# The first projection in quarters, three places of the attention stage in another order, and the last pair's down products in three parts, in a two-layer transformer kernel

## What is computed

```
mp = adaln(cond_ctx, ada_w[l], ada_b[l]);  ms = adaln(c, ada_w[l], ada_b[l])
hp = modulate(xp, norm_mix[l], mp[0], mp[1])          # hs the same with ms
qp, kp, vp, up = attn_pool_project(hp, a_w_in[i], ...)  # z = h @ w_in; q, k, v, u = split(z)
op = concatenate([attention(...), multiscale_pool(up, ...)]) @ a_w_out[i]   # or fourier_mix
xp = xp + mp[2] * op
hp = modulate(xp, norm_ffn[l], mp[3], mp[4])
xp = xp + mp[5] * hier_moe(hp, ...)
    # h1 = x@w1[e]; h3 = x@w3[e]; a = silu(h1)*h3*comb; y = sum over e of a@w2[e]
```

## Time and profile before

| | |
|---|---|
| median of 3 runs | 832.01 us (831.92 to 832.39) |
| the profiled execution: own time | 833.7 us |
| its span (first to last instruction) | 831.9 us |
| TensorE busy | 777.5 us (93%) |
| DVE, ACT busy | 328.9 us, 177.4 us |
| read from HBM | 275.04 MB |

### The profile page before, as it was taken

One profiled execution on the slowest core, in us unless ns is written; L12 is line 12 of the kernel. 1 busy time (PEld: TensorE's weight loads), 2 busy tenths in 40 slices (PEclk: granted clock), 3 DMA queues, 4 the chain that ended last, 5 costly groups with the idle time before them and its releaser, 6 DMA issues.

```text
span 831.9 us, 9943 instructions
## 1 busy us (share of the span) xinstructions
PE 777.5 (93%) x3929; PEld 380.6 (46%) x3929; DVE 328.9 (40%) x711; ACT 177.4 (21%) x422; POOL 2.2 (0%) x9
## 2 busy tenths in 40 slices
PE   3799989999899999999988999999899999999986
PEld 0454444544543444344333657645544444444332
DVE  0305047314732643445315312225832644445306
ACT  2301355403621111111112501104511101110100
POOL 0000000000000000000000000000000000000000
PEclk9899999999999999999999999999999999999999
DMA  8979599932779999999999962022499999999992
GB/s 368 400 271 428 191 430 403 422 141 85 282 269 422 420 421 420 421 421 421 422 419 427 430 278 102 1 101 112 193 354 421 421 421 421 421 421 422 420 412 86
DMA packets 39474, 277.44 MB, mean 334 GB/s; under 512 B 8525, under 2 KB 9441, under 8 KB 10497
## 3 DMA queue, kind: packets, MB, share of 16 engines
q1 hardware_dynamic: 39073, 275.28, 80.7%
q10 hardware_dynamic: 288, 1.34, 0.4%
q0 software_dynamic: 64, 0.13, 0.0%
HBM read 275.04 MB, written 1.70 MB: 333 GB/s over the span
## 4 chain that ended last, share of the span: by engine, by line
PE 83%; DMA 8%; DVE 3%; ACT 3%; issue 1%; DVEq 1%; ACTq 0%; SPq 0%
PE bank L1799 25%; PE bank L1815 12%; PE bank L1697 10%; PE bank L1993 6%; DMA ring<-in_moe_w 6%; PE bank L1784 5%; PE bank L1823 5%; PE bank L2122 4%; PE bank L1635 4%; DMA ring<-in_ada_w 2%; PE bank L2143 1%; PE bank L2061 1%; PE bank L1677 1%; PE bank L2040 1%; PE bank L1648 1%
## 5 line engine op out<-in xcount | busy, mean ns | idle before, releaser
L1799 PE MATMUL bank<-ring,Z 128*64 128x512 f32 x1024 | 229.8, 601 | 8.2 <-DMA ring<-in_moe_w 8.2
L1799 PEld LDWEIGHTS bank<-ring,Z 128*64 128x64 f32 x1024 | 75.6, 138 | 147.2 <-issue 143.7
L1815 PE MATMUL bank<-ring,Z 128*64 128x512 f32 x512 | 113.8, 596 | 0.0
L1697 PE MATMUL bank<-ring,T 128*128 128x512 f32 x192 | 83.1, 593 | 1.2 <-ACT T L1077 1.2
L1815 PEld LDWEIGHTS bank<-ring,Z 128*64 128x64 f32 x512 | 35.2, 137 | 68.9 <-issue 68.6
L1338 DVE TENSOR_TENSOR Z<-Z,bank 128x512 f32<-128x512 f32 x16 | 11.0, 688 | 138.7 <-PE bank L1799 138.7
L1635 PE MATMUL bank<-ring,cond 128*32 128x512 f32 x384 | 49.7, 645 | 8.2 <-DMA ring<-in_ada_w 7.9
L1697 PEld LDWEIGHTS bank<-ring,T 128*128 128x128 f32 x192 | 36.2, 190 | 45.6 <-issue 45.6
L1823 PE MATMUL bank<-ys,Cs 128*128 128x512 f32 x192 | 51.9, 405 | 4.4 <-DVE ys L1356 4.4
L1993 PE MATMUL bank<-ring,T 128*128 128x512 f32 (+1 forms) x144 | 53.6, 535 | 2.5 <-ACT T L888 2.5
L1369 DVE TENSOR_TENSOR x<-x,bank 128x512 f32<-128x512 f32 x84 | 52.1, 681 | 0.3
(11 more groups left out here) (224 smaller groups left out, 690.9 us busy)
## 6 DMA issues: line engine op xcount, KB each, us to landing
ring<-in_moe_w SPq DMA_DIRECT2D x192, 1024.0 KB, 15.6
ring<-in_ada_w SPq DMA_DIRECT2D x24, 2048.0 KB, 13.8
ring<-in_a_w_in SPq DMA_DIRECT2D x2, 2048.0 KB, 33.5
ring<-in_a_w_out SPq DMA_DIRECT2D x2, 2048.0 KB, 11.6
ring<-in_f_w_in SPq DMA_DIRECT2D x2, 2048.0 KB, 28.9
ring<-in_f_w_out SPq DMA_DIRECT2D x2, 2048.0 KB, 27.2
special<-in_att_const SPq DMA_DIRECT2D x1, 1792.0 KB, 9.3
x<-in_x_sample SPq DMA_DIRECT2D x2, 512.0 KB, 21.6
```

The source lines that it names most:

```text
L1697: last = pe.matmul(b[:, :], T[:, k, i * P:(i + 1) * P], w[:, k, :], start=(k == 0), stop=(k == KT - 1))
L1799: last = pe.matmul(out[BLK * u:BLK * (u + 1), :], xT[:, b, k, s0 + BLK * u:s0 + BLK * (u + 1)], w[:, k, :], start=(k == 0), stop=(k == KT ...
L1815: last = pe.matmul(psD[hh][BLK * u:BLK * (u + 1), :], aT[:, k, BLK * u:BLK * (u + 1)], w2[:, FC * hh + k, :], start=(k == 0), stop=(k == F ...
```

## The change

**The start in quarters.** The host puts the columns of `ada_w` in another order: each of the four chunks of a norm now holds shift and scale of one quarter (256) of the model's columns. After each chunk, `ada_read` on DVE does reduce, bias and gain at once for its quarter; `first_affine(j, t)` writes two of the eight column blocks of `T`, and `z_part(j, i)` does the two products that use them, in three banks that accumulate over the four quarters. The first column chunk of `a_w_in` is 512 wide (the second 256), is item 1 of the ring, and is loaded in four parts, each behind the chunk of `ada_w` with the same number; chunk 0 comes in two halves, and the two sample tiles of `x` go ahead of chunk 1. Six products on zeros that are used by nobody stand before and among the first real ones: three of 512 columns before the condition's transposes, two of 256 behind them, and two (256 and 512) around the first `ada_read`.

**The attention stage.** Chunk 4's product stands right behind `z`, ahead of the pooled branch. k is transposed and copied ahead of q, and each first score waits only for its own part of q. Chunks 7 and 8 both stand behind the first scores as before, but ACT copies chunk 7 between the two groups of `exps`; chunk 8 is read after `scores(1, 0)`; chunks 9 and 10 are read inside `values`, between transposes and products.

**The last pair.** Down products in three parts of 512, 256 and 256 columns, the third into the bank `psA`. The part-0 back products stand in the middle of part 2. DVE's and ACT's steps follow the parts. Both layers have it.

```diff
+END_PARTS = [(0, HALF), (HALF, HALF + HALF // 2), (HALF + HALF // 2, D)]
-W_IN_COLS = [256, 512, 512]
+W_IN_COLS = [512, 256, 512]
...
+            sp.dma_start(ring[:, 0, 0:SLOT // 2], before0[0][:, 0:SLOT // 2]).then_inc(ada_first, 16)
+            sp.dma_start(ring[:, 0, SLOT // 2:], before0[0][:, SLOT // 2:]).then_inc(arrived[0], 16)
+            z_part(0)
+            for t in range(1, NT):
+                sp.dma_start(x[:, t, :], x_sample[0, (t - 1) * P:t * P, :]).then_inc(x_in[t], 16)
+            for j in range(1, 4):
+                weights(j + 1, before0[j + 1])
+                z_part(j)
...
+                f, k0 = cc // 6, 2 * (cc % 6)
+                m = mcol[:, l, f, k0:k0 + 2]
+                emptied_inc(dve.tensor_reduce(m.rearrange("p k v c -> p (k v) c"), src, AX.X, ALU.add))
+                settle()
+                bias = bcol[:, (6 * l + 3 * f) * KT:(6 * l + 3 * f + 2) * KT].rearrange("p (v k) -> p k v", v=2)
+                dve.tensor_tensor(m, m, bias[:, k0:k0 + 2, :].unsqueeze(3).to_broadcast([P, 2, 2, 2]), ALU.add)
+                settle()
+                at = (R_MIX, R_FFN)[f] + l * KT + k0
+                gain = colv[:, at:at + 2].unsqueeze(2).to_broadcast([P, 2, 2])
+                dve.scalar_tensor_tensor(m[:, :, 1, :], m[:, :, 1, :], 1.0, gain, ALU.add, ALU.mult).then_inc(affine_ready, 1)
...
             exps(0, 0)
+            ada_product(7)
             exps(0, 1)
-            ada(7, 9)
+            ada_product(8)
             ada_product(9)
...
-                gated_half(s, NPAIR - 1, 2 * BLK, 0)
-                settle()
-                low_half(s, NPAIR - 1, 2 * BLK, 0)
-                last_back(0)
-                last_back(1)
-                gated_half(s, NPAIR - 1, 2 * BLK, 1)
-                last_back(2)
-                settle()
-                low_half(s, NPAIR - 1, 2 * BLK, 1)
+                end_part(gated_part, 0)
+                settle()
+                end_part(low_part_of, 0)
+                end_part(gated_part, 1)
+                last_back(0, 0)
+                end_part(low_part_of, 1)
+                last_back(0, 1)
+                end_part(gated_part, 2)
+                last_back(0, 2)
+                end_part(low_part_of, 2)
                 for i in range(NT):
-                    last_back(NT + i)
+                    last_back(1, i)
+                for i in range(NT):
+                    last_back(2, i)
                     settle()
                     dve.sem_inc(x_ready, 1)
...
+            norm_part(0, 0)
+            ada_product(0)
+            keep_warm(1, HALF // 2)
+            ada_read(0)
+            keep_warm(1)
+            z_part(0, 0)
+            norm_part(1, 0)
+            z_part(0, 1)
+            norm_part(2, 0)
+            ada_product(1)
+            z_part(0, 2)
+            ada_read(1)
+            for j in range(1, 4):
+                z_part(j, 0)
+                if j < 3:
+                    ada_product(j + 1)
+                z_part(j, 1)
+                if j < 3:
+                    ada_read(j + 1)
+                if j == 1:
+                    for i in range(NT):
+                        norm_part(i, 1)
+                z_part(j, 2)
```

More of the change, by code:

```diff
@@ L337, in scores, with values @@
             t.add(("score", i, n), "dve")
-    def values(i, half):
+    def values(i, half, between=None):
         for n in range(4 * half, 4 * half + 4):
             t.add(("PT", i, n), "act")
+        if between:
+            ada_read(between)
         if half:
@@ L1968, in moe @@
                 pair(NPAIR - 1)
+            pe.wait_ge(zeros_ready, 1)
+            for _ in range(3):
+                pe.matmul(banks[7][:, :], zeros[:, 0:P], zeros[:, P:P + HALF], start=True, stop=True)
             pe.wait_ge(small_in, loads[small_in])
@@ L1977, in _, with norm_part @@
             done_by("rows")
-            for n in range(3):
-                ada_product(n)
-                if n > 0:
-                    ada_read(n - 1)
-            norm(0, 0, 1)
-            ada_product(3)
-            ada_read(2)
-            ada_read(3)
-            for cc in range(len(W_IN_COLS)):
+            for _ in range(2):
+                pe.matmul(banks[7][:, 0:HALF // 2], zeros[:, 0:P], zeros[:, P:P + HALF // 2], start=True, stop=True)
+            def norm_part(i, q):
+                pe.wait_ge(normed, i + 1)
+                b = begin(("norm", 0, i, q))
+                for k in range(4):
+                    last = pe.transpose(b[:, k * P:(k + 1) * P], h[:, i, (4 * q + k) * P:(4 * q + k + 1) * P], ident)
+                last.then_inc(full, 1)
@@ new lines, in z_part @@
+            def z_part(j, i):
+                if j < 3:
+                    pe.wait_ge(z_weights[j], 16)
+                    w = ring[:, N_WIN[0], :].rearrange("p (k n) -> p k n", k=KT)
+                else:
+                    w = item(N_WIN[0], W_IN_COLS[0])
+                if i == 1:
+                    pe.wait_ge(first_cols["act"], j + 1)
+                else:
+                    pe.wait_ge(first_cols["dve"], 2 * j + 1 + i // 2)
+                b = begin(("z", 0, i)) if j == 0 else banks[turn[("z", 0, i)][0]]
+                for k in (2 * j, 2 * j + 1):
+                    last = pe.matmul(b[:, :], T[:, k, i * P:(i + 1) * P], w[:, k, :], start=(k == 0), stop=(k == KT - 1))
+                if j == 3:
+                    last.then_inc(full, 1)
```

345 lines of the change are left out of this document (210 added, 135 removed).

## The result

| | before | changed |
|---|---|---|
| median | 832.20 us (831.92 to 832.47, 4 runs) | 818.22 us (817.36 to 818.69, 4 runs) |
| profiled execution: own time, span | 833.7, 831.9 us | 817.36, 815.5 us |

The ratio is 0.9831, with a 95% interval of 0.9814 to 0.9848. The change made the kernel faster, and the time lies in the predicted range (811.5 to 821.5); the forecast of 816.0 was 2.2 us too low. The two profiled spans differ by 16.4 us, close to the forecast sum of 16.0, but partly by luck: one term was 4 us too large, the profiled execution of before is 1.5 us slower than its median, and that of the changed kernel (817.36) is the fastest of its four. The products on zeros that the list of the change calls six are seven: three of 512 columns, two of 256, and one each of 256 and 512.

The account below looks back on a forecast made before the run. TensorE (777.5 of 831.9 us) was taken as the bound, behind a mostly-transfer front of 34.8 us; gains 10.7 + 3.2 + 1.15 + 1.0 = 16.0 us gave 816.0 us, range 811.5 to 821.5.

Parts of the forecast that it names:

- What bounds the start: Start of the kernel: the chain begins with 18.28 us of DMA for `ada_w`; `z` starts only at 34.82 us.
- Term 1: Start in quarters: `z` ends at 78.5 us instead of 89.2, gain 10.7 us, at best 12.7, at worst 6.
- chunk 0 to 12.6 us: Start: TensorE's product of chunk 0, landed at 11.6 us, ends at 12.6, so `z_part(0, 0)` comes at 15.4 us.
- I take full clock: Start in quarters: with pauses of at most 1.6 us and products between them, TensorE is taken to run at full clock.
- the clock goes down in the quarters: Rival at the start: about 7 TensorE pauses between 8 and 26 us cost 2 to 4.5 us: 818 to 820.5; chance 0.18.
- the ring holds: Weight transfers behind the start: item 8 lands at about 55 us, wanted at about 87; nothing is late.
- the lead moves along: Whole kernel: an earlier start of TensorE's dense work moves everything behind it; the expert stream has slack to begin earlier.
- the expert stream does not move along: Rival in the experts: TensorE would wait for just-in-time transfers what it gained, giving 825 to 832 us; chance 0.03.
- Term 2: Attention stage: 4.0 us of TensorE waits removed, less 0.8 for extra DVE steps: gain 3.2 us, bounds 1.0 and 4.5.
- DVE did not become the bound: Rival in the attention stage: DVE is the bound, Term 2 falls to 0.5, time 818.7 us; chance 0.15.
- Term 3: Last pair of both layers: gain 1.15 us at layer 1's end and 1.0 us (bounds 0.3 and 2.8) after layer 0.

Follow-up runs that it names:

- more_dummies: Changed kernel with one more product on zeros ahead of the condition's copies and four instead of two behind: 815.68 us, ratio 0.9803 to the kernel before.

## Why the prediction was right, point by point

**What bounds the start** was read rightly: the transfer of the four chunks ahead of `z` was on the chain, and with quarters TensorE's own work took its place. **Term 1** was mis-sized: 10.7 us forecast, 6.7 measured. Two of its steps failed. The first is "chunk 0 to 12.6 us" and with it "I take full clock": the product ended at 14.6, at half clock, and the first part began at 17.64 instead of 15.4, 2.2 us late; more_dummies won 1.6 of them back. The prediction had assumed that pauses of at most 1.6 us are harmless, from one pause of 1.61 us in the earlier trace rows; here pauses of 0.62 and 0.89 us, with four records on zeros between them, came ahead of it. The second is the price of a part. From the start of a part that stands alone between other work to the start of what follows it, it is 1.79 to 1.88 us (17.64 to 19.43, 29.34 to 31.22), and 1.85 or 1.86 us for a chunk's product (23.36 to 25.22); the sum had 1.72 for each, the time between starts inside a long block. Six such parts cost 0.6 and three chunk products 0.4 of the remaining 1.8 us; the other 0.8 is spread over the small steps between them. Of the rival "the clock goes down in the quarters" only chunk 0 came true, at 1.6 us where its price was 2 to 4.5; the quarters themselves ran at 1.00. That the time of 818.22 us lies in that rival's 818 to 820.5 is chance, since most of what is missing in term 1 has other causes.

The products on zeros, for which the sum gave nothing, were worth 1.7 us of `z`'s end in the one execution without them. There the rule of the Trainium skill's page "TensorE: Matmul & The Clock Gate" (section "What's actually happening"), by which activity lifts the clock from its lower level, points the right way, but the place was another. The 1.3 us that the prediction drew from it for chunk 0 did not show, 3.37 us with them and 3.64 without; 1.0 us showed in the first part, where 4 records took 2.97 us without them and 1.95 with them.

The 6.7 us themselves depend on the two executions: the one of before had half clock at the start of `z`, the one of the changed kernel at chunk 0. Between the executions with the old and with the new start the lead is 4.5 to 8.2 us, and the medians' 6.6 us lie between.

**That the ring holds and that the lead moves along** was right. Every kernel kept at `project(0)` and at the experts of layer 0 what it had won, and the rival "the expert stream does not move along" fell. What the prediction left out is that the experts' time varies by 2 us from execution to execution, in part by one up step at half clock.

**Term 2** was right: 3.2 forecast, 3.7 in the two profiles, with the waits falling as named. DVE did not become the bound, although its own work grew by 3.3 us; a new wait of 0.7 us for it is all. Medians give 4.7 us, just over the upper bound of 4.5; that fits the slow stretch which followed the removed pause of 2.2 us in two of three executions.

**Term 3** was right in sum at the end of layer 1: 1.15 forecast, 1.45 between the two profiles, and 0.9 to 1.4 when the distance from the last down product to the end of the span is taken (8.45 us, against 9.37, 9.85 and 9.42 in the three executions with the old tail). For the start of layer 1 the forecast of 1.0 us names the right mechanism (TensorE is at chunk 20 2.36 us behind the last down product instead of 4.02) and leaves out the clock. With the old tail the distance to `f_w_in` was 15.12 us in the kernel before and 13.27 and 13.28 in the two others; with the new one it is mostly 13.2. TensorE comes to chunk 20 earlier, as forecast, then waits 2.2 us for the first tile, and the clock goes down behind that wait. So by the traces it is 0.1 us where the clock had held before, 1.9 us where it had not, and 0.9 us once the pause is filled.

**Why 14.0 and not 16.0.** The sum was made from the one profiled execution of before, and that execution had bad luck in layer 1: two stretches at half clock at its start (1.85 us, and 0.9 us more up to `project(1)`: 66.55 us against 65.6 in all twelve others) and 222.4 us of experts, with this up step:

```profile
801.57 8.78 PE L1799 MATMUL bank<-ring,Z 128*64 128x512 f32 x32 [3.46 <-DMA ring<-in_moe_w]
```

The changed kernel's profiled execution has the same step at 7.09 us, behind a pause of 2.37. With term 1 at 6.7, the two profiles differ by 6.7 + 3.7 + 0.4 + 1.9 + 0.9 - 0.3 + 2.2 + 0.9 = 16.4 us. Of these, 2.4 are not in the medians: 1.5 because the profile of before is above its median, and 0.9 because that of the changed kernel is below its own. The forecast had taken the sum for a difference of medians. How much the tail is worth in the median is not settled: its 2.9 us (1.4 to 3.7 by the interval) are mostly above the 1.0 to 1.5 us of the traces without a change of clock (0.1 at layer 1's start and 0.9 to 1.4 at the end), and how often the clock falls with either tail would need more profiled executions than I have.

## What to carry to other kernels

When a chain of transfers leads to one large block of products, cut the block along the contraction, so that each arriving chunk enables a part of it; then count the pieces at the price of interrupted work (here 4 to 9% more), not at the price inside a long block. Price a pause of TensorE of about 2 us at its length plus the half clock that may follow it (here up to 1.7 us, in some executions only), and put work, or even products on zeros, into pauses ahead of critical products. Before adding up a sum of small terms, ask how far the one profile that it is built on lies from the median, and at which places.

## What the runs showed that was not expected

- The clock is not decided by the program alone. With the same queue up to chunk 0, its product took 3.37, 2.78, 1.97, 3.48, 3.64, 2.96 and 3.14 us in seven profiles, the first two of the same kernel; with more products on zeros ahead, 2.04, 1.92 and 2.10; with none, 3.64. So more of them held the clock in three of three executions, against one of seven.
- The granted clock of the first 10 us does not show what the records show. PEclk is given as 1.00 there, yet the first six records of 512 columns took 5.49 us, 0.92 us each, where a record takes 0.43 us at full clock:

```profile
1.57 5.49 PE L2068 MATMUL bank<-Z 128*128 128x512 f32 x6 [1.57 <-DVE Z L1518]
```

- The experts, which are the same in all these kernels but for the last pair, took between 220.0 and 222.4 us a layer. That is more than the whole effect of the clock at the start (1.6 us), and an up step at half clock (1.3 to 1.7 us longer) is behind a part of it.
